# Eighteen weight slots for the first two expert rounds, a gather from the residual, six context products in rounds one to four, and turns inside the products

## What is computed

```python
x = x + merged @ w_out[layer]
hm = rmsnorm(x, ln_moe[layer]).reshape(B * S, D)
x = x + hierarchical_moe(hm, w_rg, b_rg, w_re, b_re, w1, w3, w2)
...
def expert_block(args):            # 64 experts in 8 groups of 8; D = 1024, hidden width 256
    xblk, e = args
    return (jax.nn.silu(xblk @ w1[e]) * (xblk @ w3[e])) @ w2[e]
```

## Time and profile before

| | us |
|---|---|
| median of three runs | 1265.73 (1264.46 to 1268.95) |
| the profiled execution | 1264.93 |
| its span, first to last instruction | 1263.1 |
| up to the start of the expert rounds | 312.7 |
| the eight expert rounds | 312.7 to 798.1 |
| embedding and the two context products | 798.1 to 845.1 |
| second block | 845.1 to 1263.1 |

### The profile page before, as it was taken

One profiled execution on the slowest core, in us unless ns is written; L12 is line 12 of the kernel. 1 busy time (PEld: TensorE's weight loads), 2 busy tenths in 40 slices (PEclk: granted clock), 3 DMA queues, 4 the chain that ended last, 5 costly groups with the idle time before them and its releaser, 6 DMA issues.

```text
span 1263.1 us, 14644 instructions
## 1 busy us (share of the span) xinstructions
PE 1190.9 (94%) x6037; PEld 824.5 (65%) x6037; DVE 310.9 (25%) x665; ACT 212.7 (17%) x437; POOL 110.6 (9%) x118
## 2 busy tenths in 40 slices
PE   6999998999999999998988888899999999999998
PEld 5887987888444535333332333688888888876687
DVE  1145349413111110110101020220001016526612
ACT  1232553203000000000000000220000000035501
POOL 0016037001000000000000000000000000125300
PEclk9999999999999999998999999999999999999999
DMA  9789322384799999999999999944444544444300
GB/s 321 263 280 325 128 100 67 101 328 165 289 406 410 411 411 417 415 417 417 418 417 419 416 420 396 306 146 146 154 159 140 167 137 164 163 144 127 99 2 34
DMA packets 149632, 323.54 MB, mean 256 GB/s; under 512 B 8671, under 2 KB 111562, under 8 KB 133194
## 3 DMA queue, kind: packets, MB, share of 16 engines
q1 hardware_dynamic: 143648, 315.27, 66.6%
q0 software_dynamic: 1536, 4.20, 1.1%
q10 hardware_dynamic: 4394, 3.31, 0.8%
HBM read 321.70 MB, written 1.05 MB: 256 GB/s over the span
## 4 chain that ended last, share of the span: by engine, by line
PE 86%; DMA 6%; ACT 2%; issue 2%; DVE 1%; POOL 1%; ACTq 0%; SPq 0%; DVEq 0%; POOLq 0%
PE bank L576 34%; PE bank L867 16%; PE bank L579 12%; PE bank L906 8%; DMA AR<-in_w 6%; PE bank L846 3%; PE bank L879 2%; PE bank L944 1%; PE bank L1003 1%; PE bank L990 1%; PE bank L882 1%; PE bank L1023 1%; PE bank L1036 1%; PE bank L747 1%; PE bank L641 1%
## 5 line engine op out<-in xcount | busy, mean ns | idle before, releaser
L576 PE MATMUL bank<-HT,ring 128*128 128x256 f32 x1760 | 384.0, 379 | 0.0
L576 PEld LDWEIGHTS bank<-HT,ring 128*128 128x128 f32 x1760 | 332.8, 190 | 44.7 <-issue 0.4
L867 PE MATMUL bank<-ring,AR 128*64 128x512 f32 x640 | 176.0, 605 | 20.5 <-DMA AR<-in_w 14.9
L867 PEld LDWEIGHTS bank<-ring,AR 128*64 128x64 f32 x640 | 55.6, 139 | 124.4 <-issue 123.8
L867 PE MATMUL bank<-AR 128*64 128x512 f32 x384 | 119.4, 613 | 0.3 <-issue 0.3
L906 PE MATMUL bank<-ring,AR 128*64 128x512 f32 x384 | 87.7, 598 | 11.3 <-ACT AR L1265 11.3
L1858 DVE TENSOR_TENSOR AR<-AR,bank 128x256 f32<-128x256 f32 x32 | 13.5, 422 | 286.0 <-ACT AR L1256 285.3
L579 PE MATMUL bank<-ring,HT 128*128 128x256 f32 (+1 forms) x384 | 81.8, 373 | 1.0 <-issue 1.0
L579 PEld LDWEIGHTS bank<-ring,HT 128*128 128x128 f32 x384 | 71.0, 190 | 10.2 <-issue 1.3
L579 PE MATMUL bank<-ring,AR 128*128 128x256 f32 x328 | 71.9, 380 | 3.2 <-DVE AR L1538 1.8
L1402 POOL TENSOR_TENSOR SM<-SM 128x2 f32<-128x2 f32 (+3 forms) x8 | 11.6, 1449 | 699.8 <-DVE SM L1520 650.6
(11 more groups left out here) (326 smaller groups left out, 1017.1 us busy)
## 6 DMA issues: line engine op xcount, KB each, us to landing
ring<-in_w SPq DMA_DIRECT2D x128, 1024.0 KB, 17.1
AR<-in_w SPq DMA_DIRECT2D x64, 1024.0 KB, 17.3
ring<-in_w_in SPq DMA_DIRECT2D x62, 1024.0 KB, 5.2
ring<-in_w_mod SPq DMA_DIRECT2D x12, 1024.0 KB, 6.2
AR<-in_w_in SPq DMA_DIRECT2D x5, 1024.0 KB, 17.1
ring<-in_w_out SPq DMA_DIRECT2D x4, 1024.0 KB, 5.1
ring<-in_w_ple_gate SPq DMA_DIRECT2D x4, 1024.0 KB, 9.5
ring<-in_w_out_conv SPq DMA_DIRECT2D x4, 1024.0 KB, 5.2
```

The source lines that it names most:

```text
L576: mm = pe.matmul(bank[:, part * T:part * T + T], w[:, k, c0 + part * P:c0 + part * P + P], act[:, k, :], start=(k == 0), stop=(k == k_n - 1))
L867: mm = pe.matmul(bank[e * SLOT:e * SLOT + SLOT, :].rearrange("p (w n) -> p w n", w=2), XG[:, k, :], w, start=(k == 0), stop=(k == DK - 1))
```

## The change

1. **Slots.** Rounds 0 and 1 use 18 slots: 12 as before, and 6 extra ones, which hold tiles 12 to 17 of round 0 and tiles 6 to 11 of round 1. `HN` is now the head of the area `AR`, so that a pair of the extra slots lies over it and over the place of two context keys; another lies over dead gates. From round 2 on there are 12. SP loads tile 16 of round 0 when the context rows have been turned (`cT`).
2. **Gather from the residual.** POOL no longer writes the normalized rows; PE gathers from `X` itself, with a step of eight floats, and the factor of the norm goes into a second selection matrix `SELR`. DVE writes four matrices a round where it wrote two.
3. **Context products.** Six stand in the rounds, one in round 1, two in 2 and 3, one in 4, and one `vc` product stays behind the embedding. Rounds 0 to 4 are written out.
4. **Turns.** `turn_hidden(p)` stands in the middle of `up(p+1)`, and the last one three quarters through `down(2)`. ACT copies the turned rows ahead of `sigmoid(p+1)`.
5. **Down tiles.** Their rows are dealt to the partitions so that each partition reads 8 KB in one piece, where it read two pieces of 4 KB; the turn picks every second column to match.

```diff
-        AR = sb("AR", [P, 25152])
+        AR = sb("AR", [P, 2048 + 25152])
+        HN = AR[:, 0:2048].rearrange("p (t d) -> p t d", t=TT)
...
-        for c in (2, 3):
-            fill(wcols(w_in2, C_V + 256 * c, 256), name="vc", feature=False)
+        fill(wcols(w_in2, C_V + 768, 256), name="vc", feature=False)
...
+        MRING = 12
+        beside = area(M0 - 2048, 6, 2048)
+        EXTRA = {0: 12, 1: 6}
+        extra_pairs = [beside[:, 4:6, :], None, AR[:, 0:4096].rearrange("p (w n) -> p w n", w=2)]
+        extra_single = [VC.rearrange("p t c -> p (t c)"), area(5120, 2048)]
...
+        def used_before(j, r):
+
+            if not (isinstance(r, int) and r < 2):
+                return r * NM + (j - MRING + 1)
+            x = extra_at(j, r)
+            if x is not None:
+                return EXTRA[0] + x + 1 if r else None
+            turns = [(q, i) for q in range(2) for i in range(NM) if extra_at(i, q) is None]
+            n = turns.index((r, j))
+            if n < MRING:
+                return None
+            q, i = turns[n - MRING]
+            return q * NM + i + 1
...
-        CTX_AT = {(0, 3): 0, (1, 1): 1, (1, 3): 2, (2, 1): 3, (2, 3): 4}
+        CTX_AT = {(1, 3): 0, (2, 1): 1, (2, 3): 2, (3, 1): 3, (3, 3): 4, (4, 3): 5}
+
+        SET = 5
...
-                    src = a["w2"][0, bass.ds(g * EPG + e, 1), :, :].rearrange("o (c p) n -> p (o c) n", p=P)
+                    src = a["w2"][0, bass.ds(g * EPG + e, 1), :, :].rearrange("o (p c) n -> p (o c) n", p=P)
...
-            for j in (4, 5, 0, 1, 2, 3, 12, 13, 14, 6, 7, 8, 9, 10, 11):
+            for j in (4, 5, 0, 1, 2, 3, 12, 13, 14, 15, 16, 17, 6, 7, 8, 9, 10, 11):
+                if MRING - RING <= j < MRING:
+                    sp.wait_ge(S("res_a"), last_result[NA - MRING + j] + 1)
+                else:
+                    sp.wait_ge(S("merged"), 4)
+                if j == 16:
+                    sp.wait_ge(S("cT"), 8)
...
-                        mm = pe.matmul(B[0][:, k * SLOT:k * SLOT + SLOT], HN[:, t, k * P:k * P + P], SEL[:, t, 0:SLOT],
+                        mm = pe.matmul(B[0][:, k * SLOT:k * SLOT + SLOT],
+                                       X[:, t, :].rearrange("p (q k) -> p k q", k=DK)[:, k, :], SELR[:, t, :],
...
+                        if k == DK // 2 and halfway is not None:
+                            turn_hidden(halfway)
...
-                        mm = pe.transpose(B[6 + p % 2][:, c * P:c * P + P], HHR[:, p % 2, c * P:c * P + P], ident)
+                        mm = pe.transpose(B[6 + p % 2][:, c * P:c * P + P], HHR[:, p % 2, :].rearrange("p (q c) -> p c q", c=2)[:, c, :], ident)
...
+                            if (e, c) == (1, 1) and late is not None:
+                                turn_hidden(late)
...
                     if p + 1 < PAIRS:
-                        up(p + 1)
-                    turn_hidden(p)
-                    down(p)
+                        up(p + 1, halfway=p)
+                    down(p, late=PAIRS - 1 if p + 2 == PAIRS else None)
...
-                    if p + 1 < PAIRS:
-                        sigmoid(p + 1)
                     act.wait_ge(S("hht_ps"), at(PAIRS, p + 1))
                     nc.scalar.activation(HHT[:, p % 2].rearrange("p c s -> p (c s)"), B[6 + p % 2][:, 0:2 * P], ACT.Copy)\
                       .then_inc(S("hht"), 1)
+                    if p + 1 < PAIRS:
+                        sigmoid(p + 1)
...
-            pool.wait_ge(S("rms"), nth("hm"))
-            for t in range(TT):
-                ins = nc.gpsimd.tensor_tensor(HN[:, t, :].rearrange("p (k q) -> p k q", k=DK),
...
-                    ins = V_.tensor_scalar(SEL[:, t, :], const("iota_slot"), POS[:, t:t + 1], None, ALU.is_equal)
+                    V_.tensor_scalar(SEL[:, t, :], const("iota_slot"), POS[:, t:t + 1], None, ALU.is_equal)
+                    ins = V_.tensor_scalar(SELR[:, t, :], const("iota_slot")[:, 0:SLOT], POS[:, t:t + 1], rs["hm"][:, t:t + 1],
+                                           ALU.is_equal, ALU.mult)
```

More of the change, by code:

```diff
@@ L459, in build @@
         NORMS = ["x", "lat", "ctx", "qk", "o", "hm", "ple", "two", "y"]
-        NORMED = [n for n in NORMS if n not in ("ple", "y")]
+        NORMED = [n for n in NORMS if n not in ("hm", "ple", "y")]
         TURNS = ["x", "ctx", "hm", "ple", "two"]
@@ L502, in _ @@
-            for j in range(MRING + len(EXTRA), NM):
-                sp.wait_ge(S("moe_used"), j - MRING + 1)
-                expert_dma(j, 0)
+                    sp.dma_start(dst.rearrange("p (k n) -> p k n", k=DK), src).then_inc(there, 16)
+            for j in (4, 5, 0, 1, 2, 3, 12, 13, 14, 15, 16, 17, 6, 7, 8, 9, 10, 11):
+                if MRING - RING <= j < MRING:
+                    sp.wait_ge(S("res_a"), last_result[NA - MRING + j] + 1)
+                else:
+                    sp.wait_ge(S("merged"), 4)
+                if j == 16:
+                    sp.wait_ge(S("cT"), 8)
+                expert_dma(j, 0, 0)
@@ L506, in context_dma @@
+            for j in range(18, NM):
+                sp.wait_ge(S("moe_used"), used_before(j, 0))
+                expert_dma(j, 0, 0)
             def context_dma(n):
                 if n < 2:
-                    sp.wait_ge(S("moe_used"), EXTRA[n] + 1)
+                    sp.wait_ge(S("moe_used"), NM + EXTRA[1] + (3, 0)[n] + 1)
                 else:
                     sp.wait_ge(S("ctx_ps"), n - 1)
-                sp.dma_start(ctx_slot(n), CTX[n][0][0]).then_inc(S(f"arr_ctx{n % 2}"), 16)
+                sp.dma_start(ctx_slot(n), CTX[n][0][0]).then_inc(S(ctx_arrived(n)[0]), 16)
@@ L953, in _ @@
             wait_emptied(of["pp"][2])
-            moe_round(FIRST, first=True)
-            for r in (1, 2):
+            moe_round(0, first=True)
+            for r in range(1, SET):
                 moe_round(r)
@@ L958, in _ @@
             pe.wait_ge(S("table"), 1)
-            rounds = pe.value_load(RT[0:1, 0:1], min_val=4, max_val=ROUNDS)
-            with pe.Fori(3, rounds) as r:
+            rounds = pe.value_load(RT[0:1, 0:1], min_val=SET + 1, max_val=ROUNDS)
+            with pe.Fori(SET, rounds) as r:
                 moe_round(r)
@@ L1277, in context @@
                 (context_keys if kind == "kc" else context_values)(c, bank).then_inc(S("ctx_done"), 1)
-            for r in range(3):
+            for r in range(SET):
                 moe_round(r)
             act.wait_ge(S("table"), 1)
-            rounds = act.value_load(RT[0:1, 0:1], min_val=4, max_val=ROUNDS)
-            with act.Fori(3, rounds) as r:
+            rounds = act.value_load(RT[0:1, 0:1], min_val=SET + 1, max_val=ROUNDS)
+            with act.Fori(SET, rounds) as r:
                 moe_round(r)
@@ L1890, in _ @@
             gathered()
-            for r in range(3):
+            for r in range(SET):
                 moe_round(r)
-            rounds = dve.value_load(RT[0:1, 0:1], min_val=4, max_val=ROUNDS)
-            with dve.Fori(3, rounds) as r:
+            rounds = dve.value_load(RT[0:1, 0:1], min_val=SET + 1, max_val=ROUNDS)
+            with dve.Fori(SET, rounds) as r:
                 moe_round(r)
```

145 lines of the change are left out of this document (71 added, 74 removed).

## The result

The change made the kernel slower, by 0.9%. The median is 1277.99 us (1276.4 to 1279.47), beside 1266.1 us for the kernel before on the same chip: a ratio of 1.0091, interval 1.0069 to 1.0113. The prediction was 1244.0 with a range of 1240 to 1256. The profiled execution took 1279.47 us, its span 1277.6.

The account below looks back on a forecast made before the run. The weight-tile queue was taken to bound the rounds, PE nearly tied; 1264.93 - 14.7 (rounds' end) - 7.0 (context product) gave 1243.2, or 1244.0 since the profiled execution lay 0.8 under the median; range 1240 to 1256.

Parts of the forecast that it names:

- The bound: In the rounds: a never-empty tile queue at 414 GB/s from 332.2 to 789.3 sets their end.
- part 3: PE in the rounds: a turn inside a product costs 0.35 us, not 0.91; PE and queue nearly tie.
- Part 1: Start of the rounds: extra slots let the queue fill from 319.8, with transfers from 322.1 instead of 332.2.
- Part 2: Tiles in the rounds: +0.5 us for a context tile, -3.6 for down tiles; last lands at 776.1, before 789.3.
- Rival A: Turns inside products cost 0.8 to 1.4 us, so PE is late in early rounds: 1250 to 1258, chance 0.14.
- D: Turns inside each up product wait for hidden rows, PE stands still: slower, 1272.7 at 2.0 us a turn; chance 0.03.
- Part 4 and 5: Last round and behind: rounds end at 783.4, -14.7 us; one context product fewer behind them, -7.0.
- the cover of the norm: Behind the rounds: the one remaining context product still covers the next block's norm, by 0.9 us.
- Part 6: Edits priced at nothing, among them the gather's step of eight: 0.1 to 0.3 us a gather, 0.1 taken.
- The rule that spoke against the edit: Gather's reads: each new 16-byte line costs, so 4-byte values step freely only up to four; eight breaks it.
- Rival B: The stepped gather is slow in every round, 6.3 us instead of 3.79: about +10 us, 1254; chance 0.08.
- E: Granted clock falling after PE waits of 3.5 us: 1.7 to 2.9 us at the very end, inside the main case.

Follow-up runs that it names:

- flat kernel: The changed kernel with its gather reading contiguous features instead of steps of eight, so features come in another order: 1245.99 us, 0.9835 of the kernel before.
- the kernel with sixteen: The change with sixteen weight slots instead of eighteen, normalized copy kept and gathered in contiguous features: 1253.51 us, 0.9896 of the kernel before.

## Why the prediction was wrong, point by point

**The bound.** That a queue with no gaps set the end of the rounds, with PE a close second, was right: the flat kernel moves 408 to 422 GB/s in rounds 1 to 6, and each tile taken from its lead costs 2.5 us or more. It was also the danger that part 3 named, "nothing is left beside it".

**Part 1, the queue fills earlier.** Right. In the flat kernel SP issues four tiles from 319.80 on, and they land at 324.7, 327.2, 329.7 and 332.1, one each 2.5 us; in the kernel before one was issued there. In the changed kernel it came 6.5 us later, at 326.26, since the first gather, ahead of the rounds, is slow as well and pushes `up(0)` back.

**Part 2, what it carries.** Right. Down tiles cost 3.2 to 4.1 us more in the old pieces (put at 3.6), and the last tile of the flat kernel lands at 777.0 (issued at 760.5, 16.5 us before), put at 776.1.

**Part 3, the turn and the balance.** Right: 0.37 us for a turn inside from contiguous columns, put at 0.35; the steps of two that part 5 of the change brings make it 0.43, which the prediction left out. The rounds of the flat kernel start at 363.8, 421.3, 485.6, 550.0 and 608.9 and end at 785.0; put were 363, 420, 484, 549, 606 and 783. Rival A has no part in the result, and D's wait doesn't appear: no turn in the changed kernel waits for the hidden rows.

**Part 4 and 5, the tail and the product behind.** -13.1 for the rounds' end in the flat kernel (785.0 against 798.1), put at -14.7; -6.9 behind it, put at -7.0, and the cover of the norm reached. With the flat gather the sum of 1244.0 stands beside 1246.0; in the changed kernel itself the rounds end at 819.55, 36 us after the 783.4 of part 4.

**Part 6 is the step that failed:** "so 0.01 each: 0.3 us a gather at most for its 32, and I take 0.1". It was 4.0 us a gather, and 1.0 to 2.3 us of lower clock in the product behind each. The row was of another kind of instruction. The turns of `X` have sixteen loads for sixteen operations, the gather thirty-two loads for sixteen, and the turns' busy time hid what the row's own loads showed. Here are these loads in the kernel before, `X` in steps of eight, then `HN` in one piece:

```profile
L603 PEld LDWEIGHTS bank<-CST,X x16: 185/193/207, 289.1 to 290.7; 128*128 128x128 f32 x16
```

```profile
L603 PEld LDWEIGHTS bank<-CST,HN x16: 139/140/142, 844.9 to 846.7; 128*128 128x128 f32 x16
```

Each load had grown from 140 to 193 ns, by 38%; the turns' pace hardly did. I divided the busy time by the count, where the duration of one load was to be read. By 38% on 3.7 us a gather would have been put at 1.4 us more, which is still not 4.0: why the same step costs a turn's load 53 ns and a gather's load 143 stays open. The rule that spoke against the edit was named and given a chance of 0.08; it should have had far more, since the only row against it came from another instruction. The sentence that the trace agrees "faintly, with 0.01 us a load" is a misreading of the same kind.

**Rival B had the mechanism and not the size.** It put 2.5 us on a gather, and 1254. It was 4.0, and B knew nothing of the clock. In E the clock was thought of only for waits of some us, as in the earlier trace rows. Here PE doesn't wait at all and still loses it: 5.87 for 3.65.

**Range and chances.** The bounds of part 6 were 0.1 to 0.3 us a gather, so its true end (9 times 6 us, an estimate from the rows above, of which 32 came out at the end) was nowhere in the range. The balance made it worse: with PE tied to the queue from round 0 on, more than half of each us on PE in the rounds came out.

## What to carry to other kernels

A price taken from a neighbouring row must come from the same instruction with the same operand in the same role; if only another kind has it, its duration one by one is to be read, and the upper bound is the worst that a rule allows. An edit that "costs nothing" and is repeated in each round deserves more care than the large terms: here ten words in an access pattern outweighed a gain of 20 us, the 1266 to 1246 of the flat kernel. When a buffer is to be given up, compare what it gives (two slots, 7.5 us in the kernel with sixteen) with what its loss makes of the reads (32 us).

## What the runs showed of the hardware

- A load of a 128x128 fp32 weight tile in a product takes 192 ns contiguous, 196 in steps of two, 261 of three, 329 of four, 335 of eight; 32 of them in a row take 3.7, 3.9, 5.6, 7.5 and 7.7 us at the shortest. In a turn (a transpose) such a load takes 139 contiguous, 206 in steps of two, 193 of eight.
- The granted clock fell to 0.50 within such a row of slow loads though PE was never idle (0.95 over a round), and did not in a row of twice as many quick ones, nor with the same slow loads dealt among long products (1.00 in both).
- Alternating at each product between `up(3)` (weight tiles of 64 columns) and the stepped gather (128 columns, another bank) took 1.62 us where the two take 0.92 apart; a single turn of 128 columns inside an up product took 0.37 us with both of its changes.
- Tiles of 1 MB in pieces of 8, 4 and 2 KB a partition: 422, 411 and 393 GB/s, the last over a whole round (a third of its expert tiles come in 8 KB); over 20 us of 2 KB pieces alone it was 392.
